# The feed-forward activations of an encoder layer, turned by VectorE and block transfers in place of TensorE

## The reference

```python
D_MODEL = 2048
D_FF = ((8 * D_MODEL + 3 * 256 - 1) // (3 * 256)) * 256     # 5632

def swiglu(x, w_gate, w_up, w_down):
    return (jax.nn.silu(x @ w_gate) * (x @ w_up)) @ w_down

xp = layer_norm(DEEPNORM_ALPHA * xp + swiglu(xp, ffn_w_gate[l], ffn_w_up[l], ffn_w_down[l]),
                ln_ffn_g[l], ln_ffn_b[l])
```

## Time and profile before

| | |
|---|---|
| median of three runs | 1915.46 us |
| profiled execution | 1916.11 us |
| its span, first to last instruction | 1914.5 us |
| mean granted TensorE clock | 0.996 |
| busy: TensorE, its weight loads | 98%, 83% |
| busy: VectorE, ScalarE, GpSimd | 56%, 38%, 10% |
| DMA | 249.98 MB, 131 GB/s over the span |
| chain that ended last | TensorE 96%, VectorE 2% |

### The profile page before, as it was taken

How to read it: one execution, slowest core, us unless ns; L and a number is a source line. 1 busy time by engine, 2 the same in 40 slices (tenths; PEclk the granted TensorE clock), 3 DMA queues, 4 the chain that set the end, 5 groups by cost and what they waited for, 6 DMA issues and landing times.

```text
span 1914.5 us, 31252 instructions
## 1 busy us (share of the span) xinstructions
PE 1885.8 (98%) x9592; PEld 1596.3 (83%) x9592; DVE 1068.9 (56%) x2419; ACT 726.3 (38%) x1466; POOL 182.6 (10%) x300
## 2 busy tenths in 40 slices
PE   7999999999999999999999999999999999999997
PEld 6999998888888888888888888888888888888886
DVE  7666666888888874564444444433334344444455
ACT  4444344444444433343333333333333333333330
POOL 2122222222222100001111110000000000000000
PEclk9999999999999999999999999999999999999999
DMA  8565564444444335344444444344444444445541
GB/s 219 154 149 154 145 168 117 110 109 107 111 111 107 111 113 164 93 128 127 133 140 127 135 122 131 125 129 129 130 128 120 135 124 125 126 128 159 180 132 66
DMA packets 241827, 249.98 MB, mean 131 GB/s; under 512 B 26872, under 2 KB 160000, under 8 KB 241120
## 3 DMA queue, kind: packets, MB, share of 16 engines
q1 hardware_dynamic: 234192, 233.60, 42.9%
q0 software_dynamic: 7568, 15.52, 3.1%
HBM read 237.67 MB, written 11.35 MB: 130 GB/s over the span
## 4 chain that ended last, share of the span: by engine, by line
PE 96%; DVE 2%; ACT 0%; issue 0%; DMA 0%; DVEq 0%; SPq 0%; POOL 0%; ACTq 0%; POOLq 0%
PE bank L293 70%; PE bank L1958 9%; PE bank L1704 7%; PE bank L1820 2%; PE bank L1201 1%; PE bank L1183 1%; PE bank L1872 1%; PE bank L1195 1%; PE bank L1177 1%; PE bank L412 0%; DVE w_lo L269 0%; DMA x_res<-in_x_prompt 0%; PE bank L1146 0%; PE bank L1244 0%; DVE stats L365 0%
## 5 line engine op out<-in xcount | busy, mean ns | idle before, releaser
L269 DVE TENSOR_TENSOR w_lo<-raw,w_hi 128x512 fp32r<-128x512 f32 (+2 forms) x828 | 563.3, 689 | 606.1 <-ACT w_hi L264 600.1
L264 ACT ACTIVATE w_hi<-raw 128x512 fp32r<-128x512 f32 (+2 forms) x828 | 501.5, 616 | 800.2 <-PE bank L293 665.1
L293 PE MATMUL bank<-w_hi,aT_hi 128*128 128x512 f32 (+2 forms) x1776 | 699.5, 394 | 4.2 <-DVE aT_lo L427 1.6
L293 PE MATMUL bank<-w_hi,aT_lo 128*128 128x512 f32 (+2 forms) x1776 | 673.8, 379 | 0.0
L293 PE MATMUL bank<-w_lo,aT_hi 128*128 128x512 f32 (+2 forms) x1776 | 672.7, 379 | 0.0
L293 PEld LDWEIGHTS bank<-w_hi,aT_hi 128*128 128x128 f32 x1776 | 334.8, 189 | 60.5 <-issue 9.7
L293 PEld LDWEIGHTS bank<-w_hi,aT_lo 128*128 128x128 f32 x1776 | 333.9, 188 | 56.1
L293 PEld LDWEIGHTS bank<-w_lo,aT_hi 128*128 128x128 f32 x1776 | 335.2, 189 | 46.6
L293 PE MATMUL bank<-w_hi,hT_hi 128*128 128x512 f32 x288 | 112.3, 390 | 0.0
L293 PE MATMUL bank<-w_hi,hT_lo 128*128 128x512 f32 x288 | 112.1, 389 | 0.0
L293 PE MATMUL bank<-w_lo,hT_hi 128*128 128x512 f32 x288 | 112.0, 389 | 0.0
(11 more groups left out here) (356 smaller groups left out, 1985.6 us busy)
## 6 DMA issues: line engine op xcount, KB each, us to landing
raw<-in_ffn_w_gate SPq DMA_DIRECT2D x176, 256.0 KB, 2.7
raw<-in_ffn_w_up SPq DMA_DIRECT2D x176, 256.0 KB, 2.7
raw<-in_ffn_w_down SPq DMA_DIRECT2D x176, 256.0 KB, 3.1
raw<-in_w_in SPq DMA_DIRECT2D x128, 192.0 KB, 2.4
raw<-in_w_in SPq DMA_DIRECT2D x128, 128.0 KB, 2.2
raw<-in_w_in SPq DMA_DIRECT2D x256, 64.0 KB, 2.2
raw<-in_w_out SPq DMA_DIRECT2D x61, 256.0 KB, 3.2
work_b<-in_cache_fox_k POOLq DMA_DIRECT2D x32, 128.0 KB, 3.8
```

Of the source, the lines that this page charges most:

```text
L264: nc.scalar.activation(w_hi[:, g % RING, 0:width], raw[:, g % RAW, 0:width], ACT.Copy).then_inc(sem("w_high"), 1)
L269: nc.vector.tensor_tensor(w_lo[:, g % RING, 0:width], raw[:, g % RAW, 0:width], w_hi[:, g % RING, 0:width], ALU.subtract).then_inc(sem("w_ ...
L293: last = nc.tensor.matmul(acc[t][:, 0:width], l[:, k0 + n, t * P:(t + 1) * P], r[:, g % RING, 0:width], start=(n == 0 and j == 0), stop=(n ...
```

## The change

In all blocks but the last of each half (nine of eleven), the twelve transposes on TensorE are left out. VectorE, right after it has written the three tiles of `hb`, transposes each within its 32x32 blocks into `sg`, which is free by then. SP then issues 16 transfers a row tile, from `sg` to `hT_lo`: each takes the 32 rows of one row block, and of each group of 128 columns one 32-column block, so 32 partitions by 4 by 32 values (rows of 128 bytes), and puts them on the partitions where they belong. The three groups of 16 stand ahead of the loads of gate pieces 11, 12 and 13 of the next block. ScalarE then copies `hT_lo` to `hT_hi`, and VectorE replaces `hT_lo` by the difference, at slots 29, 35 and 41 of that gate product (pieces 9, 11 and 13) instead of 4, 7 and 10. TensorE waits for the last of these before each down product.

The diff, cut to its core (SP's loops and the waits of the last blocks are renumbered to fit):

```diff
+MOVE_AT = (11, 12, 13)
+MOVED_AT = (29, 35, 41)
...
-            def hidden_pe(pe, j, last=False):
+            def hidden_pe(pe, half):
+                j = sum(FB[:half + 1]) - 1
...
+            def moved_blocks(half):
+
+                return sum(FB[:half]) - half
+
+            def blocks_of(x, i, t):
+
+                return x[:, bass.ds(4 * i, 4), t * P:(t + 1) * P]
+
+            def move_blocks(sp, i, m, t):
+                sp.wait_ge(sem("h_turned"), TT * (m + i) + t + 1)
+                for a in range(4):
+                    for r in range(4):
+                        sp.dma_start(
+                            hT_lo[SQUARE * r:SQUARE * (r + 1), bass.ds(4 * i, 4),
+                                  t * P + SQUARE * a:t * P + SQUARE * (a + 1)].bitcast(F32),
+                            sg[SQUARE * a:SQUARE * (a + 1), t, :].rearrange("b (k r c) -> b k r c", k=4, r=4)[:, :, r, :])\
+                            .then_inc(sem("h_moved"), 16)
+
+            def moved_act(act, i, m):
+                for t in range(TT):
+                    yield MOVED_AT[t]
+                    act.wait_ge(sem("h_moved"), 16 * 16 * (TT * (m + i) + t + 1))
+                    nc.scalar.activation(blocks_of(hT_hi, i, t), blocks_of(hT_lo, i, t).bitcast(F32), ACT.Copy)\
+                        .then_inc(sem("h_high"), 1)
+
+            def moved_dve(dve, i, m):
+                for t in range(TT):
+                    yield MOVED_AT[t]
+                    dve.wait_ge(sem("h_high"), TT * (m + i) + t + 1)
+                    nc.vector.tensor_tensor(blocks_of(hT_lo, i, t), blocks_of(hT_lo, i, t).bitcast(F32),
+                                            blocks_of(hT_hi, i, t), ALU.subtract).then_inc(sem("h_low"), 1)
...
                 dve.wait_ge(sem("h_ready"), TT * j + TT)
                 dve.sem_inc(sem("acc2_free"), TT)
+                if m is not None:
+                    for t in range(TT):
+                        nc.vector.transpose(sg[:, t, :], hb[:, t, :]).then_inc(sem("h_turned"), 1)
...
-                def up_loads(g0, j0, i, skip):
+                def up_loads(g0, j0, i, skip, half=None):
                     for n in range(skip, 2 * NP_IN):
+                        if half is not None and n in MOVE_AT:
+                            move_blocks(sp, i, moved_blocks(half), MOVE_AT.index(n))
...
-                        gate_pe(pe, g0, j0, i, Course(hidden_pe(pe, j0 + i)), ahead=1)
+                        gate_pe(pe, g0, j0, i, ahead=1)
                     up_pe(pe, g0, j0, FB[n] - 1)
                 half(0, G_UP0, 0)
+                pe.wait_ge(sem("h_low"), TT * moved_blocks(1))
...
+                pe.wait_ge(sem("h_low"), TT * moved_blocks(2))
```

More of the change, by code:

```diff
@@ L1869, in hidden_pe @@
                     pe.wait_ge(sem("h_ready"), TT * j + t + 1)
-                    pe.wait_ge(sem("h_bank"), TT * j + t + 1)
+                    pe.wait_ge(sem("h_bank"), TT * half + t + 1)
                     for k in range(4):
@@ L1874, in hidden_pe @@
                     ins.then_inc(sem("h_ps"), 1)
-                if last:
-                    yield 40
-                    pe.wait_ge(sem("h_bank"), 2 + TT * (j + 1))
+                yield 40
+                pe.wait_ge(sem("h_bank"), 2 + TT * (half + 1))
+            def moved_blocks(half):
[23 more added lines that the diff above has]
+                                            blocks_of(hT_hi, i, t), ALU.subtract).then_inc(sem("h_low"), 1)
             def hidden_act(act, i, j):
@@ L1902, in up_act, with up_dve @@
                     split_act(act, g + NP_IN + A_ACT, n, ii, per)
-            def up_dve(dve, g0, j0, i):
+            def up_dve(dve, g0, j0, i, m=None):
                 j = j0 + i
@@ L2000, in ffn_sp @@
                 with sp.Fori(0, FB[0] - 1) as i:
-                    up_loads(G_UP0 + 2 * NP_IN, 1, i, 0)
+                    up_loads(G_UP0 + 2 * NP_IN, 1, i, 0, 0)
                 with sp.Fori(0, NCB) as c:
                     down_loads(G_DN0, 0, c, NP_DN[0])
-                with sp.Fori(0, FB[1]) as i:
-                    up_loads(G_UP1, FB[0], i, 0)
+                up_loads(G_UP1, FB[0], 0, 0)
+                with sp.Fori(0, FB[1] - 1) as i:
+                    up_loads(G_UP1 + 2 * NP_IN, FB[0] + 1, i, 0, 1)
                 for c in range(NCB):
                     if c == 1:
-                        sp.wait_ge(sem("h_ps"), TT * (FB[0] + FB[1]))
+                        sp.wait_ge(sem("h_ps"), TT * 2)
                         load_gb(sp, (gb_last[:, 0, :], gb_last[:, 1, :]), ln_ffn_g[0], ln_ffn_b[0])
@@ L2021, in half @@
                         splits_beside(split_act, act, A_ACT, g0 + 2 * NP_IN, NP_IN, i, 2 * NP_IN,
-                                      Course(hidden_act(act, i, j0 + i)))
+                                      Course(moved_act(act, i, moved_blocks(n))))
                     up_act(act, g0, j0, FB[n] - 1)
                 half(0, G_UP0, 0)
-                splits_beside(split_act, act, A_ACT, G_DN0, NP_DN[0], course=Course(hidden_act(act, FB[0] - 1, FB[0] - 1)))
+                splits_beside(split_act, act, A_ACT, G_DN0, NP_DN[0], course=Course(hidden_act(act, FB[0] - 1, 0)))
                 with act.Fori(1, NCB) as c:
@@ L2028, in ffn_act @@
                 half(1, G_UP1, FB[0])
-                course = Course(hidden_act(act, FB[1] - 1, FB[0] + FB[1] - 1))
+                course = Course(hidden_act(act, FB[1] - 1, 1))
                 for n in range(len(DN1_ORDER) - A_ACT):
@@ L2041, in half @@
                     with dve.Fori(0, FB[n] - 1) as i:
-                        up_dve(dve, g0, j0, i)
+                        up_dve(dve, g0, j0, i, moved_blocks(n))
                         splits_beside(split_dve, dve, A_DVE, g0 + 2 * NP_IN, NP_IN, i, 2 * NP_IN,
-                                      Course(hidden_dve(dve, i, j0 + i)))
+                                      Course(moved_dve(dve, i, moved_blocks(n))))
                     up_dve(dve, g0, j0, FB[n] - 1)
@@ L2052, in ffn_dve @@
                 dve.wait_ge(sem("x_whole"), ROUNDS)
-                down_block(0, course=Course(hidden_dve(dve, FB[0] - 1, FB[0] - 1)))
+                down_block(0, course=Course(hidden_dve(dve, FB[0] - 1, 0)))
                 for c in range(1, NCB):
@@ L2056, in ffn_dve @@
                 half(1, G_UP1, FB[0])
-                course = Course(hidden_dve(dve, FB[1] - 1, FB[0] + FB[1] - 1))
+                course = Course(hidden_dve(dve, FB[1] - 1, 1))
                 for n in range(len(DN1_ORDER)):
@@ L2081, in ffn_pe @@
                     gemm(pe, G_DN0 + NP_DN[0] * c, NP_DN[0], hT_hi, hT_lo, 0, CW, banks, name,
-                         blk + (name == "acc2"), between=None if c else Course(hidden_pe(pe, FB[0] - 1, True)))
+                         blk + (name == "acc2"), between=None if c else Course(hidden_pe(pe, 0)))
                 half(1, G_UP1, FB[0])
-                course = Course(hidden_pe(pe, FB[0] + FB[1] - 1, True))
+                course = Course(hidden_pe(pe, 1))
+                pe.wait_ge(sem("h_low"), TT * moved_blocks(2))
                 for c in range(NCB):
```

## The result

The changed kernel takes 2082.98 us (median of four, 2080.86 to 2084.20), against 1915.36 us for the kernel before in the same comparison. The ratio is 1.0871, with a 95% interval of 1.0858 to 1.0884. It is slower, as forecast, but the forecast was 1995 us and its range ended at 2030: the loss is 168 us and not 79. The profiled execution took 2080.86 us.

What follows compares the result with a forecast made beforehand. TensorE, busy 98% of the span, was taken to bound the kernel. Per block, 8.1 us stall plus 2.1 for the clock less 1.39 for removed transposes gave 8.8; nine blocks, 79 us on 1915.5, so 1995 us, range 1932 to 2030.

Steps and rivals of the forecast that it cites:

- Added on SP: 48 moves a block at 0.566 us each ahead of load 13 in SP's stream; TensorE stalls 8.1 us a block.
- The price of the transposes on TensorE: Twelve transposes and their hand-overs cost 1.39 us a block; removing them in nine blocks gains 12.5 us.
- The deadline of load 13: Gate piece 13 is needed at 968.9, so its load must start by 964.8 us in the block worked out.
- The formula 48 p - 19.1: Stall in us a block at a move pitch of p us on SP; it is gone at p = 0.397.
- The place: One TensorE gap of 7 to 8 us at gate piece 13 in each of nine blocks, released by w_lo's split.
- The clock: TensorE's clock falls in a stall of over 7 us and costs 2.1 us a block after it; bounds 0 to 3.0.
- the row at the start: After idling from 5.4 to 12.1 us, TensorE ran 19 matmuls in 4.2 us, then 22 in 2.4 us.
- VectorE's transposes: Three a block ahead of gate piece 3's split, 0.69 us each, 2.1 us a block, hidden with 2 us in hand.
- The first (issues within the deadline): Rival: SP's issues fit before load 13's deadline; at a pitch of 0.38 us, 1903 us; chance 0.09.
- The second: Rival: SP's issues cheaper than the looped pair, no clock fall; 1938 us at 0.48, 1956 at 0.52; chance 0.14.
- the third: Rival: the stall at gate piece 13 as forecast, but TensorE's clock stays up; 1976 us; chance 0.15.
- The fourth: Rival: DMA engines, not SP, pace the moves; at 0.1 us a packet the pitch is 0.9, about 2140 us; chance 0.08.

Runs made afterwards that it cites:

- the probe: The kernel before, with 36 transfers in eight shapes issued by SP after its last output; issues in the moves' shape had a pitch of 0.641 us.
- the filled kernel: The changed kernel with 58 and 85 unread transposes on TensorE ahead of gate pieces 12 and 13 in each of nine blocks; 2064.03 us, ratio 1.0770.

## Why the prediction was wrong, and where it was right

**The step that failed** is the price of one issue on SP, in "Added on SP": 0.566 us, between 0.38 and 0.60. It measured 0.743 us, outside both bounds. The neighbouring rows were loads from device memory. What the prediction added for the loop was about right (0.12 us there, 0.10 between the probe's pitch and the moves'). What the move has and no row of before had is both ends in SBUF, and that adds some 0.2 us: 0.641 against 0.45 outside a loop, 0.743 against 0.566 in one. The text said that the trace had no such transfer, and then gave the upper bound only 0.03 us above the nearest row. With 48 of them a block, a miss of 0.177 us is 8.5 us a block and 76 us in all: 79 + 76 = 155 of the 168 us.

**The rest**, 12 us, is 1.4 us a block. From the first move to load 13 the trace has 998.23 - 960.86 = 37.4 us, where 48 x 0.743 + 1.1 gives 36.8: each change between moves and a load costs some tenths. From the start of load 13 to TensorE's start it took 4.22 us against 4.11. Together that is 0.7 us a block, 6 us. Another 3 us are spread: the profiled executions differ by 164.8 us, the medians by 167.6. In the first block TensorE waited 16.4 us instead of 15.3. What is left, some 2 us, has no cause shown.

**What held.** The price of the transposes on TensorE was foreseen as 12.5 us and measured as 13.1 with 12 issues a block. The deadline of load 13 is right: 24 issues meet it and 28 miss it. The formula 48 p - 19.1 with p = 0.743 gives 16.6 us of stall a block; the trace has 84.94 - 65.31 = 19.6 us less 2.2 for the clock, so 17.4. The place is right, gate piece 13, released by w_lo behind its load; but I had put nearly all of the stall there, and at the true pitch piece 12 waits for 7 us too. The clock was to cost 2.1 us by the row at the start, and costs 2.1 by the filled kernel, though the stalls were two and not the one that I had reckoned with: that the first costs nothing by its slow work was not foreseen. VectorE's transposes are hidden, as said, at 0.685 us against 0.69.

**The rivals.** The first (issues within the deadline) failed: 48 issues in one queue that keeps its order are 35.7 us, and one issue of 0.61 us is a third of a landing of 1.9 us. The Trainium skill, DMA: Bandwidth & Descriptors, section Issuing engines are not separate DMA queues, says that the time to initiate a DMA is usually small relative to it. The measurement decides against that rule for this change; with 12 and 24 issues a block the issues did not show in the time. The second assumed a cheaper issue and the third a clock that stays up; both went the other way. The fourth, pacing by the DMA engines, was nearest in its time and wrong in its cause: a move landed 1.9 us after its issue, and the same pieces in fewer transfers cost nothing. What it asked for, a pitch far above 0.566 us, was there, but on SP.

## What to carry to other kernels

Count the transfers that a change puts into an in-order queue, and put that time against the lead of the load behind them; here bytes and engines' shares said nothing on it. When the operation priced has an end or a kind that no row has, the nearest row is a guess and not a bound (here an issue lasted 0.608 us against 0.373 in the nearest row, 1.6 times): leave room for that, or find the number of transfers at which the answer turns and see how far off that is. A stall costs once more through the clock; in this loop that cost was only the slow work after the last wait.

## What the runs showed of the hardware that was not expected

An issue on SP with both ends in SBUF lasts 0.59 to 0.64 us (medians) in every shape tried, against 0.33 to 0.42 us with one end in device memory, and one of 384 pieces of 128 bytes lasts as long (0.608 us) as one of 128. The granted clock went to 0.50 after a wait of about 3 us, when TensorE had been at work again for 1.5 us, and came back within 4 us (28 issues a block). VectorE's transpose of 32 x 384 values, in twelve of sixteen cases from one group of 32 partitions to another, took 0.569 us, and one of 128 x 512 in place 0.685. TensorE with 1287 useless transposes finished 19 us earlier than without.
